# First normalisation's scales and biases: two broadcast transfers replaced by two rows spread by TensorE

## What is computed

```python
def layer_norm(x, g, b):
    mu = jnp.mean(x, -1, keepdims=True)
    var = jnp.mean(jnp.square(x - mu), -1, keepdims=True)
    return (x - mu) * lax.rsqrt(var + LN_EPS) * g + b

x = layer_norm(x, ln_in_g, ln_in_b)
for l in range(2):
    proj = jnp.einsum('bsd,de->bse', x, w_in[l])
    ...   # three attentions, gates, output projection, norm, feed-forward, norm
```

## Time and profile before

| | us |
|---|---|
| median of 3 runs (1503.28 to 1503.32) | 1503.31 |
| profiled execution | 1503.24 |
| its span | 1501.9 |

### The profile page before, as it was taken

The page is one execution under the profiler, slowest core; times in us unless marked ns, Lnnn a source line. Parts: engine busy times, 40 slices in busy tenths (PEclk is TensorE's granted clock), DMA queues, the critical chain, the costliest instruction groups (busy, mean ns, idle before and its releaser), DMA issues.

```text
span 1501.9 us, 18391 instructions
## 1 busy us (share of the span) xinstructions
PE 1465.2 (98%) x7191; PEld 1203.1 (80%) x7191; DVE 1003.7 (67%) x1349; ACT 785.3 (52%) x1124; POOL 64.0 (4%) x100
## 2 busy tenths in 40 slices
PE   6999999999999999999999999999999999999998
PEld 5788887788887787887778887788788888878887
DVE  5755885854457655875765555877766668777765
ACT  3565644343443555754344343686555557755553
POOL 2000000000001000000010000210000011000000
PEclk9999999999999999999999999999999999999999
DMA  8543644575565544542765665435555644555551
GB/s 316 188 162 130 243 154 139 158 236 179 186 207 168 191 131 142 185 166 85 224 217 174 191 201 168 144 115 191 180 184 168 195 152 157 159 165 182 169 184 69
DMA packets 167317, 260.99 MB, mean 174 GB/s; under 512 B 8768, under 2 KB 106720, under 8 KB 166720
## 3 DMA queue, kind: packets, MB, share of 16 engines
q1 hardware_dynamic: 166048, 252.03, 51.3%
q0 software_dynamic: 896, 6.74, 1.2%
q10 hardware_dynamic: 288, 1.05, 0.2%
HBM read 258.74 MB, written 1.05 MB: 173 GB/s over the span
## 4 chain that ended last, share of the span: by engine, by line
PE 81%; DVE 11%; ACT 4%; issue 2%; POOL 1%; DMA 1%; SPq 0%; DVEq 0%; ACTq 0%
PE ps L384 15%; PE ps L388 15%; PE ps L386 15%; PE ps L457 9%; PE ps L459 9%; PE ps L458 9%; DVE wlo L1485 4%; ACT whi L1054 2%; PE ps L988 1%; PE ps L511 1%; PE ps L534 1%; PE ps L414 1%; DVE x L1504 1%; DVE bn L1492 1%; DVE x L1502 1%
## 5 line engine op out<-in xcount | busy, mean ns | idle before, releaser
L1485 DVE TENSOR_TENSOR wlo<-raw,whi 128x2048 fp32r<-128x2048 f32 (+1 forms) x238 | 527.9, 2229 | 278.5 <-ACT whi L1054 278.2
L1054 ACT ACTIVATE whi<-raw 128x2048 fp32r<-128x2048 f32 (+1 forms) x238 | 441.7, 1865 | 209.1 <-PE ps L388 127.1
L384 PE MATMUL ps<-whi,xTh 128*128 128x512 f32 x704 | 277.8, 395 | 2.0 <-DVE gate L1878 2.0
L388 PE MATMUL ps<-whi,xTl 128*128 128x512 f32 x704 | 274.3, 390 | 0.0
L386 PE MATMUL ps<-wlo,xTh 128*128 128x512 f32 x704 | 274.2, 389 | 0.0
L457 PE MATMUL ps<-whi,xTh 128*128 128x512 f32 (+3 forms) x640 | 251.1, 392 | 8.1 <-DVE wlo L1485 2.9
L459 PE MATMUL ps<-whi,xTl 128*128 128x512 f32 (+3 forms) x640 | 242.0, 378 | 0.0
L458 PE MATMUL ps<-wlo,xTh 128*128 128x512 f32 (+3 forms) x640 | 241.5, 377 | 0.0
L384 PEld LDWEIGHTS ps<-whi,xTh 128*128 128x128 f32 x704 | 132.2, 188 | 30.7 <-DVE gate L1878 2.8
L388 PEld LDWEIGHTS ps<-whi,xTl 128*128 128x128 f32 x704 | 132.1, 188 | 27.9
L386 PEld LDWEIGHTS ps<-wlo,xTh 128*128 128x128 f32 x704 | 132.3, 188 | 26.3
(11 more groups left out here) (185 smaller groups left out, 1633.5 us busy)
## 6 DMA issues: line engine op xcount, KB each, us to landing
raw<-in_w_in SPq DMA_DIRECT2D x124, 512.0 KB, 4.7
raw<-in_w_ffn_in SPq DMA_DIRECT2D x88, 512.0 KB, 4.8
raw<-in_w_up SPq DMA_DIRECT2D x88, 512.0 KB, 4.9
raw<-in_w_ffn_out SPq DMA_DIRECT2D x44, 512.0 KB, 4.5
raw<-in_w_down SPq DMA_DIRECT2D x44, 512.0 KB, 4.6
raw<-in_w_branch SPq DMA_DIRECT2D x24, 512.0 KB, 4.6
raw<-in_w_out SPq DMA_DIRECT2D x16, 512.0 KB, 4.4
raw<-in_w_o SPq DMA_DIRECT2D x16, 512.0 KB, 4.5
```

Of the source, the lines that this page charges most:

```text
L384: PE.matmul(o, ah, hi[:, j, b], start=first and kt == 0, stop=False)
L388: mm = PE.matmul(o, al, hi[:, j, b], start=False, stop=last and j == c - 1 and i == len(kts) - 1)
L1054: AC.activation(m.whi[:, i % SPLIT, 0:w], m.raw[:, slot, 0:w], ACT.Copy).then_inc(s.w_hi, 1)
L1485: DV.tensor_tensor(m.wlo[:, i % SPLIT, 0:w], m.raw[:, slot, 0:w], m.whi[:, i % SPLIT, 0:w].bitcast(F32), ALU.subtract).then_inc(s.w_lo, 1)
```

## The change

The rows of scales and biases come as two transfers of 4 KB into partition 0 of `gate`, which is free then. VectorE sets 128 ones in partition 0 of `probT`. TensorE multiplies the ones (1 x 128, as weights) by four stretches of 512 numbers of the rows, into PSUM banks 0 to 3: every partition then has the numbers. ScalarE copies the four banks to `vec`, each adding 8 to its semaphore, so that VectorE's wait for 32 is as before. TensorE's first work is now these four products, ahead of its wait for `ident` and `rope`; of the nine identity products one is left, and all identity products go to bank 7 in place of bank 0. The 4 + 18 others stay. Later norms still take their scales and biases by broadcast transfers (lines 252 and 253).

```diff
@@ tensor_program
+    def identity_products(count):
+
+        for _ in range(count):
+            PE.transpose(ps[:, 7, 0:P], m.ident[:], m.ident[:])
+
+    PE.wait_ge(s.init, 2)
+    PE.wait_ge(s.ln_row, 32)
+    for i, c in enumerate((0, D, 512, D + 512)):
+        PE.matmul(ps[:, i, :], m.probT[0:1, 0, 0:P], m.gate[0:1, 0, c:c + 512], start=True, stop=True).then_inc(s.ln_wide, 1)
     PE.wait_ge(s.par, 32)
-
-    def identity_products(count):
-
-        for _ in range(count):
-            PE.transpose(ps[:, 0, 0:P], m.ident[:], m.ident[:])
-
-    identity_products(9)
+    identity_products(1)
@@ scalar_program
-    AC.dma_start(m.vec[:, 0:D], t["ln_g"][0:1, :].broadcast_to([P, D])).then_inc(s.vec, 16)
-    AC.dma_start(m.vec[:, D:2 * D], t["ln_b"][0:1, :].broadcast_to([P, D])).then_inc(s.vec, 16)
-    AC.wait_ge(s.init, 1)
+    AC.dma_start(m.gate[0:1, 0, 0:D], t["ln_g"][0:1, :]).then_inc(s.ln_row, 16)
+    AC.dma_start(m.gate[0:1, 0, D:2 * D], t["ln_b"][0:1, :]).then_inc(s.ln_row, 16)
+    AC.wait_ge(s.init, 2)
     AC.activation(m.small[:, 60:61], m.half[:, 0:1], ACT.Exp)
+    for i, c in enumerate((0, D, 512, D + 512)):
+        AC.wait_ge(s.ln_wide, i + 1)
+        AC.activation(m.vec[:, c:c + 512], ps[:, i, :], ACT.Copy).then_inc(s.vec, 8)
@@ vector_program
     DV.memset(m.half[:], -0.5).then_inc(s.init, 1)
+    DV.memset(m.probT[0:1, 0, 0:P], 1.0).then_inc(s.init, 1)
     DV.wait_ge(s.x_in, 16)
```

More of the change, by code:

```diff
@@ L52 @@
     "free0", "free1", "free2",
-    "x_in", "x_in2", "par", "vec", "lay", "gate_b", "gate_b2", "ln_in", "stored",
+    "ln_row", "ln_wide", "x_in", "x_in2", "par", "vec", "lay", "gate_b", "gate_b2", "ln_in", "stored",
     "init",
@@ L555, in next_bank @@
         return b
-    PE.wait_ge(s.par, 32)
     def identity_products(count):
         for _ in range(count):
-            PE.transpose(ps[:, 0, 0:P], m.ident[:], m.ident[:])
-    identity_products(9)
+            PE.transpose(ps[:, 7, 0:P], m.ident[:], m.ident[:])
[3 more added lines that the diff above has]
+        PE.matmul(ps[:, i, :], m.probT[0:1, 0, 0:P], m.gate[0:1, 0, c:c + 512], start=True, stop=True).then_inc(s.ln_wide, 1)
+    PE.wait_ge(s.par, 32)
+    identity_products(1)
     for L in range(DEPTH):
```

## The result

| | us | runs |
|---|---|---|
| before, median | 1503.42 (1503.24 to 1503.75) | 21 |
| after, median | 1506.07 (1505.73 to 1506.39) | 21 |
| ratio | 1.0017, 95% interval 1.0011 to 1.0023 | |
| after, profiled execution | 1505.79, span 1504.2 | |

The change makes the kernel 2.65 us slower by the medians; the forecast was 0.8 us faster, and the range ended at 1505.0. In short: TensorE's four spread products ran at its slow rate from the first to the last and took 7.09 us where 4.9 were forecast, and VectorE could not normalise before their copies were there.

What follows compares the result with a forecast made beforehand. TensorE bounds the span, but until 28.7 us the opening's DMA bytes and other engines set the end. The second low part at 16.4 instead of 17.15 gave -0.75 us: 1502.5 against 1503.24, range 1500.4 to 1505.0.

Steps and rivals of the forecast that it cites:

- What bounds the kernel, and that the opening carries through: Until 28.7 us transfers and other engines set the end, then TensorE; an opening shorter by d shortens the program by d.
- What the change removes: Opening DMA: 1.05 MB less 8 KB ahead of the first weight pieces, which land 2.8 us sooner.
- (a) the landing: Bias row's transfer in the opening: issued at 1.16, landed at 4.2 us, bounds 2.9 to 5.4.
- (b) the four products: TensorE's spread: 4.9 us, slow for the first 2.8 us, then fast; bounds 3.5 and 6.9; drain 0.16 more.
- (c) and (d): ScalarE's last piece copy, 0.60 us plus 0.03 to 0.04 per signal; VectorE's extra memset, costing nothing.
- T: Moment VectorE may begin to normalise, after all four spread pieces: 9.9 us forecast, 8.74 before; break-even 10.65.
- From T to the chain: VectorE from first normalising to second low part: 6.5 us without waits, so 16.4 against 17.15.
- the first: Slow products: TensorE stays slow through all four spread products, 6.9 us, T = 11.9, program 1504.5 us; chance 0.22.
- two misfortunes: Slow spread products with rows landing at 5.4 besides: T = 13.1, program 1505.7 us; no separate chance given.
- The third rival: Freed DMA carried whole: rows at 2.9, fast products, second weight piece binds, -2.8 us, 1500.4; chance 0.13, whole or most.
- The second rival: Late rows: landing at 5.4 behind x's packets, products as forecast, T = 11.1, +0.45 us, 1503.7; chance 0.08.
- the fourth: Head start eaten before the end by a later load or GpSimd's slow root, 1503.2 us; chance 0.05.

Runs made afterwards that it cites:

- one row: Kernel before with its nine identity products replaced by three f32 products using one row of x; 1505.58 us, single execution.
- all rows: Kernel before with its nine identity products replaced by three f32 products using all 128 rows of x; 1503.51 us, single execution.
- no transfer: Kernel before without the two spread transfers, vec filled with ones and zeros by VectorE; 1501.64 us.
- nine again: Changed kernel with nine identity products behind the spread instead of one; 1505.41 us.
- warm 8: Changed kernel with eight full-height products of ones on TensorE ahead of its wait for the rows; 1506.08 us.
- halves: Changed kernel with VectorE's wait for the spread rows split, first quarter after two pieces, second after four; 1504.41 us.
- warm 8, halves: Changed kernel with eight full-height products ahead of the rows and VectorE's wait split in two; 1504.37 us.
- warm 12, halves: Changed kernel with twelve full-height products ahead of the one-row spread and VectorE's wait split in two; 1502.91 us.
- full height: Changed kernel with spread products on all 128 rows, the other 127 zero, rows landing in partition 127; 1504.80 us.
- full height, warm 8, halves: Changed kernel with a full-height spread, eight full-height products ahead and VectorE's wait split in two; 1502.90 us.
- full height, warm 12, halves: Changed kernel with a full-height spread, twelve full-height products ahead and VectorE's wait split in two; 1503.05 us.
- the same with warm 8, no extra semaphore: Changed kernel with full-height spread, eight full-height products ahead and split wait, the zeroing of gate counting on init; 1502.72 us.

## Why the prediction was wrong

**What bounds the kernel, and that the opening carries through**: right. The distance of 2.18 us at the second low part was 2.18 at the transposes and 2.35 at VectorE's last instruction.

**What the change removes**: 2.5 us by the kernel without the transfers, for a forecast of 2.8 (by the median of ten runs 1.9). x came at 4.26, for a forecast of 5.0. Both were hidden by the wait for the rows, as the forecast said that they would be in part.

**(a) the landing**: 4.57 for 4.2, from issue at 1.27: 3.3 us. It lay between the bounds of 2.9 and 5.4. By the fixed cost of the Trainium skill (page "DMA: Bandwidth & Descriptors", section "Anatomy of one DMA — SWDGE (gpsimd) path") it would have been 3.2 on the clock. That section gives its 2.0 us for transfers that GpSimd issues, and ScalarE issued these, so the forecast stretched the figure; measured here, the row took 3.3 us from issue to landing.

**(b) the four products**: this is the step that failed: 7.09 us for 4.9. The price of a product at the slow rate was right (1.77 us measured, 1.73 forecast), and the 0.43 us between records in the kernels that got fast is that of the fast rate. The rise after 2.8 us was taken from full-height identity products and put on products of one row. The text named that difference, but gave the case 0.22, and in the sum it wrote "one row or 96 rows I cost alike". They are alike in time at a given rate, and not in what they do to the rate. Even for full-height work 2.8 us (2.9 by the record of the clock) was the shortest seen: the runs had 4.0 us for the three products on x, 4.8 for the changed kernel's own transposes (14.05 to 18.90), and 6.0 with the full-height spread. The forecast also set the doubling against a granted clock that "reads 1.00 throughout"; there was no such contrast, since nothing is recorded ahead of 11.43. The Trainium skill's statement ("TensorE: Matmul & The Clock Gate", "What's actually happening") that the number of slow matmuls differs between runs of one kernel is borne out: with the same products from the same moment, 1.33 us, the clock rose at 4.34 in one kernel and at 5.93 in the other, which differ only in the semaphore on which a memset counts.

**(c) and (d)**, the copy and the signals, 0.60 and 0.04, and the memset: right.

**T** was 12.46 for 9.9, the break-even being 10.65.

**From T to the chain**: 6.87 us for 6.5. The extra 0.37 is the second piece's copy, which waited for the transposes at the slow rate. The text had "0.4 more at TensorE's slow rate", and judged that it would still be in time; the slack was 0.4 by its own numbers, and the transposes, their drain and the signals together used more. It also counted dropping eight identity products as free. Putting them back was worth 0.5 us up to the second low part, and 0.3 to 0.4 after it.

The sum: -0.75 forecast, plus 0.37 (landing), 2.19 (products) and 0.37 (slow transposes) is 2.18, which is what the trace has. The rest to 2.65 is 0.17 on the way to the end and the part outside the span.

**The rivals**: the first was what happened, with its sign and its mechanism, at 1504.5 for 1506.07. It was priced with the landing and the transposes of the forecast, and so were the 1505.0 of the range and even the 1505.7 of two misfortunes. A slow TensorE is one cause with two effects, and the second was left out of that rival's price. The third rival, the freed transfers carried whole, needed the fast rate from the start; with eight full-height products ahead and a full-height spread the second low part started at 14.99, for that rival's 14.35. The second rival and the fourth did not happen: the rows were 0.37 us late, and the distance at the transposes was still there at the end.

## What to carry to other kernels

A product with one row is a cheap-looking way to spread numbers over partitions, but it took as long as a full one, and in these traces it neither raised TensorE's rate nor kept it. At the start of a program price it at the slow rate (1.7 us for 512 f32 columns here), or give it all rows and put full-height work ahead. Before giving up transfer bytes for work on an engine, place that work on the chain: here 2.5 us of bytes were exchanged for 7.9 us between the rows' landing and their first use (4.57 to 12.46), and VectorE had to spare only the 1.9 us up to T = 10.65. And when a consumer needs the pieces one after another, let it wait for them one after another; that alone was worth 1.4 us in the span and 1.7 by the medians. Where a profile prints a granted clock of 1.00 at the very start of a program, check it against the spacing of the products.

## What the hardware showed that was not expected

- One-row f32 products back to back for 7.1 us left TensorE at the slow rate, and during one-row products a fast TensorE fell back, 2.4 us after the last full-height product, while 128 rows of which 127 held zeros raised it.
- The trace records the granted clock only from its first change, and the views print 1.00 ahead of it. In all fourteen profiles the first record begins where the spacing falls (0.85 to 0.43 us a record of 512 columns, 0.21 to 0.11 of 128). Later falls are recorded, and read 0.50.
- The rise has no fixed delay. It came 2.9 to 6.3 us after full-height work began (counted from the last pause of over 1.5 us or of one-row work):

| kernel | full-height work from, us | rise, us | delay, us |
|---|---|---|---|
| before | 8.53 | 11.43 | 2.9 |
| changed | 14.05 | 18.90 | 4.8 |
| one row | 13.82 | 18.56 | 4.7 |
| all rows | 6.03 | 10.01 | 4.0 |
| no transfer | 5.62 | 11.94 | 6.3 |
| nine again | 11.85 | 15.89 | 4.0 |
| warm 8 | 14.30 | 19.59 | 5.3 |
| halves | 11.81 | 17.40 | 5.6 |
| warm 8, halves | 11.91 | 16.78 | 4.9 |
| warm 12, halves | 1.07 | 4.57 | 3.5 |
| full height | 4.69 | 10.66 | 6.0 |
| full height, warm 8, halves | 1.33 | 5.93 | 4.6 |
| full height, warm 12, halves | 1.33 | 7.44 | 6.1 |
| the same with warm 8, no extra semaphore | 1.33 | 4.34 | 3.0 |

- With eight full-height products ahead (3.7 us of work), the same kernel gave two groups of times 3.3 us apart.
- The last output transfer took 2.6 us to land in nine profiles, 3.1 in the one-row kernel with twelve products ahead, and 3.8 in the four full-height ones. In these five an instruction packet was moved beside it, in the nine none; that it is the cause is not shown.
